# Seven block products in place of eight for the first four k tiles of gate and up

## What is computed

```
D_FF = 5632
h = rms_norm(x, norm_ffn_pre[l])
f = (jax.nn.silu(h @ w_ffn_gate[l]) * (h @ w_ffn_up[l])) @ w_ffn_down[l]
x = x + rms_norm(f, norm_ffn_post[l])
```

## Time and profile before

| | us |
|---|---|
| median of 3 runs | 2297.91 (2297.87 to 2298.04) |
| the profiled execution | 2298.06 |
| its span | 2296.4 |
| PE busy in the span | 2285.4 |
| DVE busy | 1443.3 |
| ACT busy | 1172.7 |

### The profile page before, as it was taken

How to read it: one execution, slowest core, us unless ns; L and a number is a source line. 1 busy time by engine, 2 the same in 40 slices (tenths; PEclk the granted TensorE clock), 3 DMA queues, 4 the chain that set the end, 5 groups by cost and what they waited for, 6 DMA issues and landing times.

```text
span 2296.4 us, 27501 instructions
## 1 busy us (share of the span) xinstructions
PE 2285.4 (100%) x10741; PEld 1916.4 (83%) x10741; DVE 1443.3 (63%) x1902; ACT 1172.7 (51%) x1535; POOL 25.6 (1%) x35
## 2 busy tenths in 40 slices
PE   9999999999999999999999999999999999999998
PEld 7888888888888888888888888888888888888887
DVE  6677777756666645555455555675677756576864
ACT  6555655444445744444444444465555456556443
POOL 0000000000000000000000000000000000000000
PEclk9999999999999999999999999999999999999999
DMA  8566665766667566666666666656565665656553
GB/s 296 177 194 200 193 187 172 225 202 204 192 203 273 171 200 208 202 207 210 195 203 203 201 195 221 228 180 190 168 179 171 206 216 153 198 159 184 173 200 135
DMA packets 258578, 452.03 MB, mean 197 GB/s; under 512 B 23601, under 2 KB 63537, under 8 KB 257809
## 3 DMA queue, kind: packets, MB, share of 16 engines
q1 hardware_dynamic: 258016, 449.74, 62.7%
q10 hardware_dynamic: 432, 0.53, 0.1%
HBM read 434.99 MB, written 2.10 MB: 190 GB/s over the span
## 4 chain that ended last, share of the span: by engine, by line
PE 97%; DVE 2%; ACT 1%; DMA 0%; SPq 0%; issue 0%; DVEq 0%; ACTq 0%
PE pm L993 30%; PE pm L995 30%; PE pm L994 30%; PE pb L681 1%; PE pb L863 1%; DVE wl L2246 1%; PE pb L761 1%; PE pb L771 0%; DVE yR L1788 0%; DMA raw<-in_w_in 0%; ACT wh L1500 0%; PE pm L988 0%; PE pm L987 0%; PE pm L982 0%; PE pm L986 0%; PE pm L981 0%
## 5 line engine op out<-in xcount | busy, mean ns | idle before, releaser
L2246 DVE TENSOR_TENSOR wl<-raw,wh 128x1024 fp32r<-128x1024 f32 (+3 forms) x786 | 947.8, 1210 | 739.0 <-ACT wh L1500 736.7
L1500 ACT ACTIVATE wh<-raw 128x1024 fp32r<-128x1024 f32 (+3 forms) x786 | 819.2, 1046 | 899.7 <-PE pm L995 894.8
L993 PE MATMUL pm<-wh,hTh 128*128 128x512 f32 x702 | 275.2, 392 | 1.1 <-DVE wl L2246 1.1
L993 PE MATMUL pm<-wh,x2Th 128*128 128x512 f32 x704 | 273.9, 389 | 0.0
L994 PE MATMUL pm<-wl,x2Th 128*128 128x512 f32 x704 | 273.9, 389 | 0.0
L995 PE MATMUL pm<-wh,x2Tl 128*128 128x512 f32 x704 | 273.9, 389 | 0.0
L995 PE MATMUL pm<-wh,hTl 128*128 128x512 f32 x702 | 273.3, 389 | 0.0
L994 PE MATMUL pm<-wl,hTh 128*128 128x512 f32 x702 | 273.3, 389 | 0.0
L993 PE MATMUL pm<-wh,xT3h 128*128 128x512 f32 (+1 forms) x640 | 249.0, 389 | 0.0
L995 PE MATMUL pm<-wh,xT3l 128*128 128x512 f32 (+1 forms) x640 | 244.6, 382 | 0.0
L994 PE MATMUL pm<-wl,xT3h 128*128 128x512 f32 (+1 forms) x640 | 244.4, 382 | 0.0
(11 more groups left out here) (427 smaller groups left out, 3160.4 us busy)
## 6 DMA issues: line engine op xcount, KB each, us to landing
raw<-in_w_in SPq DMA_DIRECT2D x286, 512.0 KB, 3.7
raw<-in_w_ffn_gate SPq DMA_DIRECT2D x88, 512.0 KB, 4.3
raw<-in_w_ffn_up SPq DMA_DIRECT2D x88, 512.0 KB, 4.0
raw<-in_w_ffn_down SPq DMA_DIRECT2D x88, 512.0 KB, 4.1
raw<-in_w_o SPq DMA_DIRECT2D x64, 512.0 KB, 4.3
raw<-in_w_in SPq DMA_DIRECT2D x68, 256.0 KB, 3.3
raw<-in_w_branch_b SPq DMA_DIRECT2D x32, 512.0 KB, 3.9
raw<-in_w_out SPq DMA_DIRECT2D x32, 512.0 KB, 4.7
```

The costliest lines, as they stand in the source:

```text
L993: e.matmul(o, ah[:, kk, t], h[:, c], start=first, stop=False)
L1500: e.activation(h[:, 0:n], r[:, 0:n], ACT.Copy).then_inc(s["hi"], 1)
L2246: e.tensor_tensor(l[:, 0:n], r[:, 0:n], h[:, 0:n].bitcast(F32), ALU.subtract).then_inc(s["lo"], 1)
```

## The change

In blocks 1 to 10 the first four k tiles of gate and up are taken together as one product of 2x2 blocks: rows are the two token halves (`early`, `late`), the inner dimension is the pair of k tiles (0, 1) or (2, 3), and columns are the two matrices. Strassen's form (Winograd's) needs seven block products instead of eight. A new group `fs{c}` comes before `fg{c}`, which now begins at k tile 4, as does `fu{c}`; block 0 stays as it was. Each of the seven products is a slab of one step with six matmuls, in this order: b11, b21, t1, t3, b22, t2, t4. Its weights take a slot of `wh` and `wl` each. The four `t` weights are differences of loaded ones: DVE subtracts in place in the `raw` buffers, each time right behind the low part of b11, b21, t1 and t3. The four loads of a group `fs` can be replaced only after t2, t3, t4 and b22.

The products go to `pb4` (b11), `pb5` (t1), `pb7` (t3), `pb6` (t2), and b21, b22 and t4 straight into the accumulators of fg (`pm1`) and fu (`pm0`), where the plain k tiles are added. ACT copies b11 to `C11`; DVE adds up `C12`, `C21`, `C22`. At the end of fg DVE adds `pm1` to C11 and C21 and ACT takes Silu from there; at the end of fu DVE adds `pm0` to C12 and C22 and multiplies them into `fst`. The left-hand sums of activations (`sform`) are made once, during fg0.

```
+FORMS = ("b11", "b21", "t1", "t3", "b22", "t2", "t4")
+BLOCK = {"b11": 0, "t1": 0, "t2": 0, "t3": 1, "b21": 2, "t4": 2, "b22": 3}
+SUMS = {"b11": ("t1", 0, 1, 0), "b21": ("t3", 1, 3, 1), "t1": ("t2", 0, 3, 0), "t3": ("t4", 2, 2, 0)}
...
         for c in range(c0, c0 + n):
-            add(f"fg{c}", "x2T", a["w_ffn_gate"][0], 512 * c, ev=("a", 2))
-            add(f"fu{c}", "x2T", a["w_ffn_up"][0], 512 * c)
+            if c:
+                seven(f"fs{c}", "x2T", w_g, w_u, 512 * c, range(4))
+            kts = range(4 if c else 0, 16)
+            add(f"fg{c}", "x2T", w_g, 512 * c, kts=kts, ev=("d" if c else "a", 2))
+            add(f"fu{c}", "x2T", w_u, 512 * c, kts=kts)
...
+            for k in range(2):
+                cols = slice(512 * k, 512 * k + 512)
+                e.matmul(out, lhs[0][k], h[:, cols], start=(k == 0), stop=False)
+                e.matmul(out, lhs[0][k], l[:, cols], start=False, stop=False)
+                ins = e.matmul(out, lhs[1][k], h[:, cols], start=False, stop=bool(b) and k == 1)
+            ins.then_inc(s["mm"], 1)
...
+    def gathered(c):
+
+        n = 4 * c - 4
+        yield p.end[f"fs{c}"]
+        w.wait_ge(s["mm"], p.first[f"fs{c}"] + 6)
+        w.wait_ge(s["q_c"], c)
+        w.wait_ge(s["f_s"], 2 * c - 2)
+        e.tensor_tensor(m.C12[:, :], m.C11[:, :], m.pb[6][:, :], ALU.add).then_inc(s["q_d"], 1)
+        w.wait_ge(s["q_d"], n + 1)
+        e.tensor_tensor(m.C21[:, :], m.C12[:, :], m.pb[7][:, :], ALU.add).then_inc(s["q_d"], 1)
+        e.tensor_tensor(m.C12[:, :], m.C12[:, :], m.pb[5][:, :], ALU.add).then_inc(s["q_d"], 1)
+        w.wait_ge(s["q_d"], n + 2)
+        e.tensor_tensor(m.C22[:, :], m.C21[:, :], m.pb[5][:, :], ALU.add).then_inc(s["q_d"], 1)
+
+    def joined(name, halves, value):
+
+        yield p.end[name]
+        w.wait_ge(s["mm"], p.end[name])
+        w.wait_ge(s["q_d"], value)
+        for half, C in enumerate(halves):
+            e.tensor_tensor(C[:, :], C[:, :], banks(name)[:, half, :], ALU.add).then_inc(s["ev_d"], 1)
...
-        if g.swap:
+        i = p.load_of[j]
+        r, h, l = m.raw[i % NRAW], m.wh[p.slot[j]], m.wl[p.slot[j]]
         w.wait_ge(s["hi"], p.split[j])
+        if g.pair:
+            e.tensor_tensor(l[:, :], r[:, :], h[:, :].bitcast(F32), ALU.subtract).then_inc(s["lo"], 1)
+            if kts[0] in SUMS:
+                q = i - BLOCK[kts[0]]
+                _, into, x, y = SUMS[kts[0]]
+                R = [m.raw[(q + b) % NRAW][:, :] for b in range(4)]
+                for b in (into, x, y):
+                    w.wait_ge(s[f"raw{(q + b) % NRAW}"], p.loaded[q + b])
+                w.wait_ge(s["sums"], p.sums[j])
+                e.tensor_tensor(R[into], R[x], R[y], ALU.subtract).then_inc(s["sums"], 1)
```

More of the change, by code:

```diff
@@ L182, in __init__, with load @@
         self.g = {g.name: g for g in groups}
+        self.plain = [g for g in groups if not g.pair]
+        self.acc = {g.name: i % 2 for i, g in enumerate(self.plain)}
+        self.before = {g.name: b for g, b in zip(self.plain[2:], self.plain)}
         self.first, self.end, self.evac, self.slabs, self.slab_at = {}, {}, {}, [], []
-        self.split, self.loaded = [], []
-        n, ev, ops, landed = 0, {"a": 0, "d": 0}, 0, [0] * NRAW
+        self.split, self.loads, self.loaded, self.load_of, self.sums = [], [], [], [], []
+        self.freed = []
+        n, ev, ops, sums, landed = 0, {"a": 0, "d": 0}, 0, 0, [0] * NRAW
+        def load(g, cols, kts):
+            slot = len(self.loads) % NRAW
+            self.loads.append((cols, kts, g.n))
+            landed[slot] += 16 * len(cols)
+            self.loaded.append(landed[slot])
+            self.freed.append(None)
         for g in groups:
             self.first[g.name] = n
+            if g.pair:
+                q, half = len(self.loads), len(g.kts) // 2
+                for kts in (g.kts[:half], g.kts[half:]):
+                    for cols in g.pair:
+                        load(g, cols, kts)
+                for form in FORMS:
+                    j = len(self.slabs)
+                    self.slabs.append((g, (form,), n))
+                    self.slab_at.append(j)
+                    self.load_of.append(q + BLOCK[form])
+                    self.freed[q + BLOCK[form]] = j
+                    n += 1
+                    ops += 1
+                    self.split.append(ops)
+                    self.sums.append(sums)
+                    sums += form in SUMS
+                self.end[g.name] = n
+                continue
             at = 0
@@ L603, in sync_program @@
     step = 0
-    for j in range(NRAW, len(p.slabs)):
-        while p.ahead(step) < j - NRAW:
+    for j in range(NRAW, len(p.loads)):
+        while p.ahead(step) < p.freed[j - NRAW]:
             step += 1
@@ L925, in background, with seven @@
             yield from layer(l)
+    def seven(g, n):
+        c, of_a, of_b = int(g.name[2:]), p.g["fg" + g.name[2:]], p.g["fu" + g.name[2:]]
+        act, k0 = m.acts[g.act], g.kts[0]
+        A, B = m.pm[p.acc[of_a.name]], m.pm[p.acc[of_b.name]]
+        early, late = slice(0, 128), slice(128, T)
+        for i, form in enumerate(FORMS):
+            j = p.slab_at[n + i]
+            h, l = m.wh[p.slot[j]], m.wl[p.slot[j]]
+            w.wait_ge(s["lo"], p.split[j])
+            if form == "b11":
+                out, lhs, b = pb[4][:, :], [[x[:, k0 + k, early] for k in range(2)] for x in act], 4
+            elif form == "b21":
+                out, lhs, b = A[:, 0, :], [[x[:, k0 + 2 + k, early] for k in range(2)] for x in act], None
+                before = p.before[of_a.name]
+            elif form == "b22":
+                out, lhs, b = B[:, 0, :], [[x[:, 3, k, :] for k in range(2)] for x in m.sform], None
+                before = p.before[of_b.name]
+            elif form == "t4":
+                out, lhs, b = A[:, 1, :], [[x[:, k0 + 2 + k, late] for k in range(2)] for x in act], None
+            else:
+                b, f = {"t1": (5, 0), "t2": (6, 1), "t3": (7, 2)}[form]
+                out, lhs = pb[b][:, :], [[x[:, f, k, :] for k in range(2)] for x in m.sform]
+            if b:
+                free(b)
+                bank[b] = ("q_c", c) if b == 4 else ("q_d", 4 * c)
+                w.wait_ge(s["s_l"], 1)
+            elif form != "t4":
+                w.wait_ge(s[f"ev_{before.ev[0]}"], p.evac[before.name])
+            for k in range(2):
[4 more added lines that the diff above has]
+            ins.then_inc(s["mm"], 1)
     w.wait_ge(s["warm"], 1)
@@ L932, in tensor_program @@
     n = 0
-    for i, g in enumerate(p.groups):
-        acc = m.pm[i % 2]
+    for g in p.groups:
+        if g.pair:
+            while due <= n:
+                due = next(bg, p.steps)
+            seven(g, n)
+            n += len(FORMS)
+            continue
+        acc = m.pm[p.acc[g.name]]
+        joined = g.name[:2] in ("fg", "fu") and g.kts[0]
         layer_of = int(g.name[2:3]) if g.act in ("xT3", "qlT", "kvT") and g.name[:2] != "uk" else 0
@@ L992, in tensor_program @@
                     o = acc[:, half, 0:g.n]
-                    e.matmul(o, ah[:, kk, t], h[:, c], start=first, stop=False)
+                    begun = joined and (half == 0 or g.name[:2] == "fg")
+                    e.matmul(o, ah[:, kk, t], h[:, c], start=first and not begun, stop=False)
                     e.matmul(o, ah[:, kk, t], l[:, c], start=False, stop=False)
@@ L1003, in tensor_program @@
     g = p.g[LAST]
-    acc = m.pm[p.groups.index(g) % 2]
+    acc = m.pm[p.acc[LAST]]
     for i, k in enumerate(g.kts):
@@ L1449, in background @@
             for c in range(c0, c0 + n):
-                yield p.end[f"fg{c}"]
+                if c:
+                    yield p.first[f"fs{c}"] + 2
+                    w.wait_ge(s["mm"], p.first[f"fs{c}"] + 1)
+                    e.activation(m.C11[:, :], m.pb[4][:, :], ACT.Copy).then_inc(s["q_c"], 1)
+                else:
+                    yield from forms_high()
+                yield p.end[f"fg{c}"] + (c > 0)
                 w.wait_ge(s["rstd"], RS["r0"])
```

119 lines of the change are left out of this document (89 added, 30 removed).

## The result

| | us |
|---|---|
| before, median of the runs beside it | 2297.89 (2297.83 to 2298.04) |
| the changed kernel, median of 4 runs | 2333.54 (2331.69 to 2335.58) |
| ratio | 1.0155, 95% interval 1.0138 to 1.0173 |
| forecast | 2310.6 (2303 to 2319) |
| span of the profiled execution, before and after | 2296.4, 2331.3 |

What follows compares the result with a forecast made beforehand. TensorE, busy 2285.4 of 2296.4 us, was taken as the bound. Block-start losses net of savings, 5 x 2.31 + 2 x 1.43 + 0.22 - 0.90 - 1.06 = 12.7 us, gave a median of 2310.6 us, range 2303 to 2319.

Steps and rivals of the forecast that it cites:

- What goes: First two gate and up slabs of ten blocks: seven products replace them, saving 1.36 us per block, 13.6 in all.
- Junctions without backlog: Block starts: PE waits 0.69 us before t3 and 2.1 before b22, net +1.43; less at blocks 1, 6, 9.
- Backlog: Starts of blocks 2, 3, 4, 5, 8: late crossing delays DVE, t3's wait becomes 1.57 us, net +2.31 each.
- Mid-block: Plain slabs: low part behind the four adds ends at 34.8, wanted at 34.97; just in time, no wait.
- rival (2): Mid-block waits too, since cover there is 0.1 us; time 2318.2 us; chance 0.10.
- upper bound: Crossing lands a microsecond later: mid-block low part misses by 0.95 us in eight blocks, +7.6 us, 2318.2.
- rival (5): PE's clock falls to 1.2 GHz for three products behind the second block-start wait: 33 us more, 2343; chance 0.04.
- rival (3): Faster: if b22's low part ended by T+5.4, PE never waits, all 13.6 us won, 2284.3; chance 0.04.

Runs made afterwards that it cites:

- e5: Changed kernel, arithmetic kept, b22 last of the seven products and small steps (joins, transpose, gather, crossing) moved to where inputs are ready; 2286.4 us, ratio 0.9951.
- e3: Changed kernel without the four weight subtractions in a block, so t1 to t4 use plain weights; 2314.7 us, ratio 1.0073.
- e4: Changed kernel with only the old block's transpose moved from before b22's low part to behind t2's; 2321.3 us, ratio 1.0105.
- e1: Changed kernel with b11's copy, the gather and the gate-end adds put ahead of the previous block's fT parts; 2306.1 us, ratio 1.0038.
- e7: Changed kernel with b11's copy and the gather put ahead of the fT parts, which keep their steps; 2312.2 us, ratio 1.0063.
- e8: Changed kernel with the fT parts moved behind the gate block's end and b11's copy ahead of them, gather at its old place; 2305.9 us, ratio 1.0035.
- e9: Changed kernel with loads of plain gate and up slabs in blocks 1 to 10 halved to one k tile; 2315.5 us, ratio 1.0077.
- e2: Changed kernel with only SP's crossing transfers due two steps earlier; 2318.6 us, ratio 1.0090.

## Why the prediction was right and wrong, by its steps

**What goes.** Right: 1.36 us per block, shown by the length of a block in e5 (42.17 to 42.19 for 43.52).

**Junctions without backlog.** Right in place, order and size. Before t3 0.57 for 0.69, before b22 1.9 for 2.1. Block 1 waits 1.40 for 1.58. Block 6 is 0.90 us shorter, block 9 is 1.07 us shorter, where 0.90 and 1.06 were forecast. e3 and e4 show the two largest terms one by one: the subtractions, and the transpose with 1.13.

**Backlog.** Right in place (blocks 2, 3, 4, 5 and 8) and near in size, 1.11 to 1.62 us for 1.57. That it comes from the gather standing behind the late parts is shown by e1, e7 and e8: where the two are parted, all seven waits are 0.57 to 0.64. The rest of its path, through the gate-end adds and Silu, fits but was not tested alone. The junction waits together are 23.0 us where the forecast had 12.7 + 13.6 = 26.3.

**Mid-block: this step failed.** The prediction took SP's last transfer out at T+24.6, "ACT starts the fT part 1.9 later", and found the low part behind the gather "just in time, no wait in mid-block", with 0.1 us of cover. The first `fT` operation starts at T+27.1 to 30.9, not at 26.5. Three things in it were off:
- The 1.9 (1.84 by its rows) was read from a stretch in which the DMA engines were busy 0.65 of their time, and used for one in which loads held back for ten microseconds come together with the 16 transfers. There it is 3.2 to 6.2. e9 takes the bytes away and has 1.8. This is the main term, 13.2 of 17.5 us.
- The walk was made for one block. SP's last transfer is out at T+23.4 to 25.6 in the eight blocks, as summed in most, and 0.4 to 1.0 us later in three (3, 5, 8). In e9, where the transfer is fast again, these three have 1.7 us of the 4.3. Another 1.7 are in blocks 1, 7 and 10: PE waited less at their start, and so wants the low part 0.8 to 2.0 us sooner. Block 2, whose transfer still took 2.9 us, has 0.8. Block 4 has SP at T+24.6, the transfer at 1.8, and no wait: there the sum comes out.
- It followed the late parts only to the gather, so that rival (2) had one wait of 0.95 us per block. But the part that waits for the transfer itself stands ahead of a low part, and holds DVE idle for 5.9 us. So there are two waits in most blocks, 1.4 to 2.8 us in all, and rival (2) had 7.6 us for the middle where 17.5 were lost.

A cover of 0.1 us under a sum of four resources should have had the larger share of the chances, not the 0.10 of rival (2), and its upper bound should have been worked out for a transfer that meets full DMA engines.

**Not in the sum at all:** the restarts, 32 of 0.11 us, 3.5 us. They were in the rows: the matmul at 13.26 in the earlier trace rows is listed with 0.50 where others have 0.39.

**Clock, rival (5).** The form is right, the size far smaller. The spacing goes from 0.227 to 0.427 for some eight matmuls, twice in the run, which is 1.2 in place of 2.4 GHz: after the 2.8 us wait of block 2 and after the 1.62 and 1.91 us of block 8. Together 3.3 us, where the rival had 33. The stretch of the second, with a granted clock of 0.67 on average over its 5 us (columns as above), and the timeline of PE in the first:

```profile
1248.00:1253.00 5.00, 5.00 (x17) 3.92 (x16) 3.56 (x4) 2.33 (x3) 0.00 (x0) 0.67 0.90 286
```

```profile
922.28 0.50 PE L1085 MATMUL pm<-wh,x2Th 128*128 128x512 f32 x1 [2.65 <-DVE wl L2428]
...
923.31 0.39 PE L1086 MATMUL pm<-wl,x2Th 128*128 128x512 f32 x1
923.54 0.59 PE L1087 MATMUL pm<-wh,x2Tl 128*128 128x512 f32 x1
923.93 0.63 PE L1085 MATMUL pm<-wh,x2Th 128*128 128x512 f32 x1
924.35 0.63 PE L1086 MATMUL pm<-wl,x2Th 128*128 128x512 f32 x1
...
927.07 0.40 PE L1086 MATMUL pm<-wl,x2Th 128*128 128x512 f32 x1
927.31 0.40 PE L1087 MATMUL pm<-wh,x2Tl 128*128 128x512 f32 x1
```

The rule of the Trainium skill named there ("TensorE: Matmul & The Clock Gate", "A second HAM failure mode: psum-queue depth-cycling") holds here only for these two stretches: the other 28 waits of the run, up to 1.91 us long, left the spacing as it was. e2 and e3 had one such stretch each, e3 after a wait of 2.29 us, e2 in block 7 after 0.57 and 1.91. The changed kernel has these same two waits in its blocks 7 and 10, without a fall. The other kernels had none, though e1 has 17 waits of up to 1.9 us. Why the one wait brings it on and the other of the same length does not stays open.

**Faster, rival (3).** It asked that the low part of b22 end by T+5.4, and had 0.04. e5 does not shorten DVE's work: it lets b22 be wanted at T+8.2 instead. The rival was worked out for the order as it stood, which is what the changed kernel has.
